# A two-block kernel: the order of its opening, and who computes and folds the modulation chunks

## What is computed

```python
c_act = jax.nn.silu(c)
for l in range(DEPTH_2):                      # DEPTH_2 = 1
    mod = (c_act @ ada_w[l] + ada_b[l])[:, None, :]
    sh1, sc1, g1, sh2, sc2, g2 = jnp.split(mod, 6, axis=-1)
    h = rmsnorm_2(x, norm1_g[l]) * (1.0 + sc1) + sh1
    x = x + g1 * hybrid_mixer(h, ...)
    ...
```

## Time and profile before

| | |
|---|---|
| median of three runs | 2453.67 us |
| the profiled execution | 2456.84 us, its span in the trace 2455.0 us |
| TensorE busy | 2308.2 us, 94% of the span |
| VectorE, ScalarE, GpSimd busy | 922.9, 855.3 and 899.3 us |
| mean granted TensorE clock | 0.982 of full speed |

### The profile page before, as it was taken

One profiled execution on the slowest core, in us unless ns is written; L12 is line 12 of the kernel. 1 busy time (PEld: TensorE's weight loads), 2 busy tenths in 40 slices (PEclk: granted clock), 3 DMA queues, 4 the chain that ended last, 5 costly groups with the idle time before them and its releaser, 6 DMA issues.

```text
span 2455.0 us, 29917 instructions
## 1 busy us (share of the span) xinstructions
PE 2308.2 (94%) x11831; PEld 1520.6 (62%) x11831; DVE 922.9 (38%) x1479; ACT 855.3 (35%) x1584; POOL 899.3 (37%) x395
## 2 busy tenths in 40 slices
PE   6999999999999998989899898999999999999996
PEld 5677777876777787778787685444444444444442
DVE  6555643125655355255434642122222222222223
ACT  5344454533455443543334742122222112121111
POOL 5566666866666586864333470000000000000000
PEclk9999999999999999999999998999999999999998
DMA  9676666686766661432223329999999999999995
GB/s 373 254 301 277 274 248 236 228 327 250 282 275 267 271 228 69 172 137 87 87 103 123 118 89 402 424 427 427 428 430 428 428 429 428 428 429 428 428 428 241
DMA packets 60725, 718.64 MB, mean 293 GB/s; under 512 B 11072, under 2 KB 11680, under 8 KB 16720
## 3 DMA queue, kind: packets, MB, share of 16 engines
q1 hardware_dynamic: 58720, 714.35, 71.3%
q10 hardware_dynamic: 1904, 2.86, 0.3%
HBM read 712.94 MB, written 4.24 MB: 292 GB/s over the span
## 4 chain that ended last, share of the span: by engine, by line
issue 39%; PE 16%; DVE 3%; ACT 2%; DMA 1%; DVEq 0%; POOLq 0%; POOL 0%; ACTq 0%
PE bank L379 5%; PE bank L433 2%; PE bank L389 2%; PE bank L443 1%; DMA weight_ring<-in_w_in_dram 1%; PE bank L518 1%; PE bank L524 1%; PE bank L621 1%; ACT w_hi_parts L2510 1%; PE bank L522 1%; PE bank L481 0%; PE bank L482 0%; PE bank L479 0%; PE bank L472 0%; PE bank L365 0%
## 5 line engine op out<-in xcount | busy, mean ns | idle before, releaser
L2183 POOL TENSOR_TENSOR weight_ring_parts<-weight_ring,w_hi_parts 128x1024 fp32r<-128x1024 f32 (+2 forms) x368 | 871.7, 2389 | 542.3 <-ACT w_hi_parts L2510 540.8
L2510 ACT ACTIVATE w_hi_parts<-weight_ring 128x1024 fp32r<-128x1024 f32 (+2 forms) x368 | 376.6, 1041 | 440.4 <-PE bank L2274 160.8
L1504 POOL TENSOR_TENSOR rms_out<-rms_in,minus_half 128x2 f32<-128x2 f32 x2 | 1.4, 696 | 967.5 <-DVE rms_in L1850 954.3
L1587 PE MATMUL bank<-weight_ring,qk_t 128*64 128x512 f32 x1024 | 230.8, 607 | 15.8 <-DMA weight_ring<-in_expert_w_up_dram 15.8
L2263 PE MATMUL bank<-w_hi_parts,h_t_parts 128*128 128x512 f32 (+1 forms) x768 | 215.0, 404 | 12.1 <-ACT w_hi_parts L2510 10.5
L2274 PE MATMUL bank<-weight_ring_parts,h_t_parts 128*128 128x512 f32 (+1 forms) x768 | 194.3, 382 | 8.8 <-POOL weight_ring_parts L2183 8.8
L2263 PE MATMUL bank<-w_hi_parts,x_res_parts 128*128 128x512 f32 (+1 forms) x768 | 199.1, 383 | 0.0
L1587 PEld LDWEIGHTS bank<-weight_ring,qk_t 128*64 128x64 f32 x1024 | 78.3, 140 | 165.5 <-issue 165.5
L2263 PEld LDWEIGHTS bank<-w_hi_parts,h_t_parts 128*128 128x128 f32 x768 | 133.7, 191 | 58.1 <-issue 27.6
L2274 PEld LDWEIGHTS bank<-weight_ring_parts,h_t_parts 128*128 128x128 f32 x768 | 140.2, 189 | 37.7 <-POOL weight_ring_parts L2183 9.2
L2263 PEld LDWEIGHTS bank<-w_hi_parts,x_res_parts 128*128 128x128 f32 x768 | 141.0, 189 | 29.9
(11 more groups left out here) (476 smaller groups left out, 3583.0 us busy)
## 6 DMA issues: line engine op xcount, KB each, us to landing
weight_ring<-in_w_in_dram SPq DMA_DIRECT2D x63, 2048.0 KB, 7.6
weight_ring<-in_ada_w_dram SPq DMA_DIRECT2D x48, 2048.0 KB, 12.1
weight_ring<-in_expert_w_gate_dram SPq DMA_DIRECT2D x32, 2048.0 KB, 26.9
weight_ring<-in_expert_w_up_dram SPq DMA_DIRECT2D x32, 2048.0 KB, 18.3
weight_ring<-in_expert_w_down_dram SPq DMA_DIRECT2D x32, 2048.0 KB, 24.0
weight_ring<-in_w_out_dram SPq DMA_DIRECT2D x24, 2048.0 KB, 7.8
proj<-in_expert_w_gate_dram SPq DMA_DIRECT2D x16, 2048.0 KB, 26.8
proj<-in_expert_w_up_dram SPq DMA_DIRECT2D x16, 2048.0 KB, 16.5
```

What stands on the lines that cost most here:

```text
L1587: last = mm(bank[side][s, :], m.xg[:, 8 * j + k, s], weights(hu + e, 8)[:, k, :], start=j == 0 and k == 0, stop=j == 1 and k == 7)
L2183: nc.gpsimd.tensor_tensor(weights(split, True), weights(split, False), rounded(split).bitcast(f32), ALU.subtract)\
L2510: A_(rounded(split), weights(split, False), ACT.Copy).then_inc(w_hi_ready, 1)
```

## The change

It has five parts.

- GpSimd takes pieces 0 to 7 of the first unit, all eight, before its first power; before, it took three. ScalarE rounds pieces 5 to 7 before the first half of the squares (before: piece 4), piece 8 between the two halves of the squares and piece 9 behind them. Piece 8 is the first of unit 1.
- SyncE loads the first half of unit 1's weights between the first and the second modulation half of chunk 0. In layer 0 the weights of the latent up-projections (`uq`, `ukv`) are loaded behind unit 1's modulation halves instead of unit 0's.
- `c_2` is loaded second on ScalarE's queue instead of last, has a semaphore of its own, and goes through Silu in the middle of the rounding of x. The first dummy activation is Silu instead of Square.
- VectorE gets the products of chunk 3 in layer 0 and of chunks 1 and 3 in layer 1; TensorE did them.
- The fold of VectorE's chunks 0 to 5 moves from between the units into the next unit, ahead of the `by_hi` of its piece 1. That of chunk 0 in layer 0 goes ahead of piece 6 (the seventh). Chunk 6 stays.

```diff
-BY_VECTOR = ((0, 2, 4, 5, 6), (2, 4, 5, 6))
+BY_VECTOR = ((0, 2, 3, 4, 5, 6), (1, 2, 3, 4, 5, 6))
+FIRST_FOLD = 6
+FOLD_AT = {0: 1, 1: 1, 2: 1, 3: 1, 4: 1, 5: 1}
...
-        for key in HALVES.order:
+        order = HALVES.order
+        for key in order[0:3] + [order[4], order[3], order[5]] + order[6:]:
...
-                if s == 0 and j == 1:
+                if (l, s, j) in ((0, 1, 1), (1, 0, 1)):
...
-            split_to(q + (X_AT[3][1] if l else 0) + AHEAD)
+            split_to(q + (X_AT[3][1] + AHEAD if l else FIRST[1] - 1))
             root(0, 2)
...
-            pe.wait_ge(td_copied, td.now())
             if p not in BY_VECTOR[l]:
+                pe.wait_ge(td_copied, td.now())
...
-            else:
-                pe.wait_ge(ada_used, 24 * l + 2 * p + 2)
-                nc.tensor.matmul(psTD[0:1, :], half[:, 0:1], ada_sum, start=True, stop=True).then_inc(row_summed, 1)
+                td.next()
+            elif p not in FOLD_AT:
+                fold(l, p)
+
+        def fold(l, p):
+
+            pe.wait_ge(td_copied, td.now())
+            pe.wait_ge(ada_used, 24 * l + 2 * p + 2)
+            nc.tensor.matmul(psTD[0:1, :], half[:, 0:1], ada_sum, start=True, stop=True).then_inc(row_summed, 1)
             td.next()
...
+                if u - 1 in BY_VECTOR[l] and u - 1 in FOLD_AT:
+                    later = sorted([(FOLD_AT[u - 1] if l + u > 1 else FIRST_FOLD, lambda: fold(l, u - 1))] + later, key=lambda x: x[0])
                 unit(l, u, later, bank_free)
...
+        act.dma_start(ccol[:, :], a["c_cols"]).then_inc(in_c, 16)
...
-        A_(m.osq[:, 0:8], half[:, :], ACT.Square)
+        A_(m.osq[:, 0:8], half[:, :], ACT.Silu)
...
                 for j in range(8):
                     first_rounded(j)
                     split_to(min(j, 2))
-                split_to(4)
+                    if j == 4:
+                        act.wait_ge(in_c, 16)
+                        A_(ccol[:, :], ccol[:, :], ACT.Silu).then_inc(setup_a, 1)
+                split_to(7)
                 first_squares(0)
-                split_to(5)
+                split_to(8)
                 first_squares(1)
-                split_to(6)
-                act.wait_ge(in_pos, 48)
-                A_(ccol[:, :], ccol[:, :], ACT.Silu).then_inc(setup_a, 1)
+                split_to(9)
...
-                split_to(q + sum_place(p) + AHEAD)
+                split_to(q + (sum_place(p) if l + p else FIRST[1] + FIRST_FOLD - 1) + AHEAD)
                 store_row(l, p)
```

More of the change, by code:

```diff
@@ L2030, in program @@
     x_rows = PROJ[:, :, 0:D]
-    first_in, rows_x_in, x_lo_ready = sem("first_pieces_in"), sem("x_rows_in"), sem("x_remainder")
+    in_c, first_in, rows_x_in, x_lo_ready = sem("c_col_in"), sem("first_pieces_in"), sem("x_rows_in"), sem("x_remainder")
     small = lambda l, at, n: small_all[:, l * SMALL + at:l * SMALL + at + n]
@@ L2491, in _ @@
                       a["positions"].rearrange("(a n) -> a n", a=1).partition_broadcast(P)).then_inc(in_pos, 16)
-        act.dma_start(ccol[:, :], a["c_cols"]).then_inc(in_pos, 16)
         act.wait_ge(half_ready, 1)
-        A_(m.osq[:, 0:8], half[:, :], ACT.Square)
+        A_(m.osq[:, 0:8], half[:, :], ACT.Silu)
         act.wait_ge(in_small, 16)
@@ L2758, in _ @@
         dve.wait_ge(in_cst, 16)
-        dve.wait_ge(in_pos, 48)
+        dve.wait_ge(in_pos, 32)
         prow = PB[:, 0, 0, :]
```

## The result

The changed kernel takes 2463.76 us (median of 8 runs, 2460.02 to 2467.11), the kernel before beside it 2456.26 us (8 runs, 2448.24 to 2458.55). The ratio is 1.0033, with a 95% interval of 1.0019 to 1.0047: slower by 8 us, between 4.7 and 11.5, where +7.0 was forecast.

The account below looks back on a forecast made before the run. TensorE, busy 94% of the span, bounds the kernel. Opening -1.4, chunk 1 of layer 1 -2.6, chunk 3 of both layers +8.0 and half clock +3.0 sum to +7.0: 2460.7 us, range 2450 to 2467.

Parts of the forecast that it names:

- The opening: Start of layer 0 through unit 2's start: 3.1 us kept, 1.7 lost to half clock, so -1.4 us (-4.5 to +1.5).
- chunk 1 of layer 1: Products moved to VectorE in layer 1: TensorE saves a 3.55 us product, pays a 0.95 us fold, -2.6 us.
- chunk 3 of both layers: Unit 3 and its following fold: stretched rotations delay VectorE, TensorE stands 6.6 us; +8.0 plus 3.0 us half clock.
- T: Time origin for unit 3 of layer 0: the end of the up-projections, 106.45 us in the earlier trace.
- Rival 1: Unit 3: GpSimd keeps its gaps, rotations are not stretched, TensorE stands 2.4 us; -3.4 us, 2450.3; chance 0.17.
- Rival 2: Opening: unit 2's weights come in time, so -8.2 us instead of -1.4, the rest as forecast; 2453.9; chance 0.12.
- rival 3: Opening pays in full and rotations in unit 3 are not stretched: -10.2 us, 2443.5; chance 0.06.
- Rival 4: Unit 3: rotations are stretched in only one layer; +1.8 us, 2455.5; chance 0.10.
- The half clock at unit 2: After TensorE's stand of about 5 us in front of unit 2, slow running costs 1.7 us.
- The half clock at chunk 3's folds: After the 6.6 us stand at that fold, slow running costs 1.5 us in each layer (0 to 1.7).
- The load of unit 1's first half: Opening: its weight transfer, with a backlog again, lands between 35.6 and 37.9 us, taken as 37.0.
- L: Landing time of the first half of unit 1's weights, taken as 37.0; chunk 0 starts 4.6 us later.

Follow-up runs that it names:

- The opening alone: Changed kernel with chunk 3 of both layers and chunk 1 of layer 1 back on TensorE, folds as before except layer 0's chunk 0: 2453.79 us.
- the bank: Changed kernel with the rotations' cosines, sines and intermediate in a free PSUM bank, so each rotation has one SBUF input: 2445.82 us, ratio 0.9961.
- ScalarE ahead: Changed kernel with ScalarE rounding four more pieces of unit 3 before it waits for chunk 2's row: 2452.17 us, ratio 0.9983.
- squares ahead: Changed kernel with both halves of the squares ahead of piece 8's rounding: 2456.88 us, ratio 1.0003.

## Why the prediction was right

**The three terms, measured.** The opening alone -2.0 us (forecast -1.4), chunk 1 of layer 1 alone -3.9 (-2.6), chunk 3 of both layers +13.5 (+11.0). Only two of the three are measured apart from the change: chunk 3's is the change less the kernel without it, so the sum of +7.6 against the measured +8 tests one thing, that the opening and chunk 1, -5.9 together, bring what the kernel without chunk 3 has, -5.4. Nothing large lies between the parts. The chunk 3 term is good to some 4.4 us either way; no term is shown to be wrong.

**Where the trace has them.** TensorE's shift can be read at its modulation steps that are in both kernels. Before:

```profile
216.87 1.02 PE L2318 MATMUL bank<-ada_sums,minus_half 128*1 128x512 f32 x2
...
506.25 3.61 PE L2313 MATMUL bank<-weight_ring,c_col 128*1 128x512 f32 x32
531.77 3.61 PE L2313 MATMUL bank<-weight_ring,c_col 128*1 128x512 f32 x32
566.86 1.02 PE L2318 MATMUL bank<-ada_sums,minus_half 128*1 128x512 f32 x2
```

After:

```profile
220.77 1.02 PE L2327 MATMUL bank<-ada_sums,minus_half 128*1 128x512 f32 x2
...
509.79 3.61 PE L2316 MATMUL bank<-weight_ring,c_col 128*1 128x512 f32 x32
537.08 1.02 PE L2327 MATMUL bank<-ada_sums,minus_half 128*1 128x512 f32 x2
567.91 1.02 PE L2327 MATMUL bank<-ada_sums,minus_half 128*1 128x512 f32 x2
597.46 1.87 PE L2327 MATMUL bank<-ada_sums,minus_half 128*1 128x512 f32 x2 [6.47 <-DVE ada_sums L2974]
```

- Opening: the up-projections end at 106.70 - 1.9 = 104.8 instead of 106.45, so -1.6. The sum had -1.4.
- Chunk 3 of layer 0: chunk 6's fold, which isn't moved, has 220.77 - 216.87 = +3.9, so chunk 3 brought +5.5. The sum had 4.0 + 1.5 = +5.5. In it the rotations' end at T + 18.6 was forecast at T + 18.7 (five held), the stand of 6.37 at 6.6. They were not the five forecast: GpSimd began at T + 5.8, not T + 6.5, and so held the last of the larger rotations (110.74) and four of the smaller six.
- Chunk 1 of layer 1: +3.5 at chunk 0's product (509.79 - 506.25); then the product would have ended, with the `by_hi` behind it, at 531.77 + 3.55 + 1.95 = 537.3, and the fold in its place ends at 537.08 + 0.95 = 538.0: +0.8. That is -2.8, where the sum had -2.6, and no wait stands there.
- Chunk 3 of layer 1: another stand of 6.47 us, and the half clock again. Chunk 6's fold there stands at +5.8 (683.03 against 677.28). With the -0.9 ahead of it (below) chunk 3 brought +6.7, 0.63 of it the new wait at that fold; the sum had 5.5. At the start of the second block the shift is 5.5 us, at the end of the span 3.8; where the 1.7 us between go isn't known.

**Rivals.** Rival 1 (the rotations not stretched) is excluded by the five operations of 2.4 us and the stand. The kernel with the fold of chunk 2 back comes near to what it describes (GpSimd keeps its gaps, three rotations held), and it gives back 17.4 us. Rival 2 (the opening pays in full) falls with unit 2's start at 72.01 and with the opening alone, and rival 3 (both) with either. Rival 4 (one layer only) falls with the second stand.

**Terms that were mis-sized**, though each sum held:
- The half clock at unit 2. The sum had 1.7 us, from the 3 us at half clock in the earlier trace rows. That stretch was in fact 6.8 us long, 3.8 of them while TensorE stood:

```profile
32.00:35.80 3.80, 0.00 (x0) 0.00 (x0) 1.92 (x7) 3.75 (x8) 3.04 (x3) 0.50 0.95 397
35.80:38.80 3.00, 2.98 (x7) 2.40 (x8) 2.86 (x4) 1.62 (x3) 3.00 (x2) 0.50 1.04 406
```

  In front of unit 2 it was 6.8 us again (71.5 to 78.3), but only 0.5 of it fell into the stand. It cost 3.0 us: of the lead of 2.9 us with which unit 2 starts nothing is left at its end. That the opening still came out at -1.6 is luck, by something that the prediction didn't have: the kernel before has a stretch of 3.4 us at half clock at 90, in the up-projections, and the changed kernel has none there. Before, then after:

```profile
90.00:93.00 3.00, 3.00 (x4) 1.45 (x5) 2.86 (x5) 0.95 (x1) 0.00 (x0) 0.50 1.01 431
```

```profile
90.00:93.00 3.00, 2.94 (x7) 1.44 (x8) 2.88 (x4) 0.50 (x2) 3.00 (x3) 1.00 0.87 367
```

  In layer 1 it is the same: before has such a stretch at 550.8, after doesn't, which takes the shift from +0.8 to -0.9 (567.91 - 1.9 = 566.0 against 566.86). What puts these stretches there stays open, and not every execution has them. The kernel with chunk 1 of layer 1 alone, whose first layer is that of before, has none at 90 and 13.7 us of half clock from 27.9 instead.
- The half clock at chunk 3's folds also lasted 6.8 us each, 1.87 - 1.02 us of it on the fold alone. Here the term of 1.5 held in layer 0, as the sum of 5.5 shows.
- The load of unit 1's first half: unit 0 ended at 35.3 (38.27 - 3.00), not 37.1, and so the load was issued at 26.2, not 28.0; but it was 10.8 us on its way, not 9.0. Two errors of 1.8 us cancel at L = 37.0, which is luck. TensorE's stand of 3.00 us at 38.27, which the prediction didn't have, is covered by the stand in front of unit 2: nothing of unit 1 decides when that starts. Behind the backlog the transfer took longer than both loads of `w_in` in the earlier trace rows (9.9 and 7.6 us). The two modulation halves issued at 48.0, when nothing was moving, and at 54.3 took 7.5 and 7.4 us. The Trainium skill (DMA: Bandwidth & Descriptors, Anatomy of one DMA) has a fit, measured on the path of GpSimd's queue, that would give an estimate of 6.8 us for any of these; none agrees, and for the last two the row of 7.6 us was the better base.

**How far one execution can be trusted for the opening.** Six profiled kernels have the changed opening and the same code up to the end of the up-projections: after, and those with chunk 3 back, chunk 2's fold back, the bank, ScalarE ahead, and the opening alone. In them unit 2 starts between 70.65 and 72.96, and the up-projections end between 102.7 and 105.5; in the two with the opening of before they end at 106.45 and 106.75. So the opening brings between 0.9 and 4 us, and the forecast of 1.4 is within that, on the low side.

**The port.** The Trainium skill (SBUF — State Buffer, SBUF: two separate sides) calls the port pair that VectorE and GpSimd share an exclusive lock: between a VectorE operation with two SBUF inputs and a GpSimd operation that reads SBUF, whichever starts first keeps it for the whole instruction. The rotations agree: beside the same five pieces of GpSimd they take 2.4 us each with two SBUF inputs, and 0.29 to 0.42 with one of the two in PSUM.

## What to carry to other kernels

When two engines exclude each other, the number of operations that are held hangs on whether the longer one's work has gaps: a shift of 2 us that removes gaps of 0.2 us can hold two more operations for 2.4 us each (five instead of three here), so lay both engines' rows side by side after each shift, not their busy sums. Put one operand of the short operations into PSUM ahead of any rescheduling. And before a stall in the opening is removed, follow the next load that depends on it through the issuing engine's order: the time was found again where small loads that weren't yet needed stood ahead of the weights that were.

## What was not expected of the hardware

How long TensorE ran at a granted clock of 0.50 around a stand didn't follow from the stand. In the changed kernel it was 6.8 us at each stand of 3.0 to 6.5 us (at 38, in front of unit 2, at both folds of chunk 3). In the other kernels a stand of 4.50 us (unit 2, chunk 3 given back) and one of 4.32 us (unit 2, squares ahead) had 3.4 us. One of 2.81 us (chunk 3's fold of layer 1, ScalarE ahead) and one of only 1.83 us (before unit 1, chunk 3 given back) had 3.4 us too. One of 2.82 us (before unit 1, chunk 2's fold back) and one of 1.55 us (chunk 3's fold of layer 0, ScalarE ahead) had none. What a stretch costs hangs on how much of it passes while TensorE stands anyway: with 3.8 of 6.8 us in the stand it was 1.6 us (before, at 32), with 0.5 it was 3.0 (after, at 71.5). These are single stretches of profiled executions, not a rule. A transfer of 2 MB took 7.5 us with nothing else moving and 10.8 us behind a backlog. The gaps of GpSimd that let a second VectorE operation pass were as short as 0.18 us (layer 1, ScalarE ahead); at one of 0.17 us in layer 0 none did.
